# The further slots of split expert weights placed at a multiple of 128 bytes in the partition instead of 64 past one

## The chip, the core and the metric

One program runs on one core of one Trainium2 chip. The metric is the device time of one execution in microseconds (us); smaller is better. The kernel before took 1519.38 us, the median of three runs (1519.09 to 1523.42).

## What is computed

The reference is one inference step of a two-layer decoder: 256 prompt tokens and 8 sample tokens, model width 1024, all in float32. Layer 0 is a gated linear recurrence and a dense SwiGLU; layer 1 is a short convolution and a SwiGLU of 8 experts, of which each token takes 2. The change touches the experts alone:

```python
def moe_swiglu(x, router, w1, w3, w2):
    logits = (xt @ router).astype(F32)
    top_v, top_i = lax.top_k(logits, TOP_K)
    gates = jax.nn.softmax(top_v, axis=-1)
    combine = jnp.sum(jax.nn.one_hot(top_i, N_EXPERTS, dtype=F32) * gates[..., None], axis=1)
    for e in range(N_EXPERTS):
        out = out + combine[:, e:e + 1] * swiglu(xt, w1[e], w3[e], w2[e]).astype(F32)
```

with `swiglu(x, w1, w3, w2) = (silu(x @ w1) * (x @ w3)) @ w2`. w1 and w3 are 1024 x 3584 for each expert, w2 is 3584 x 1024.

## The kernel before

**Products in three parts.** Every large product is made of three TensorE products of fp32r numbers. A weight w is split into a high part (`whi`, an fp32r copy that ScalarE writes) and a low part (`wlo`, w minus the high part, which VectorE writes); the activations are split in the same way (`xgh` and `xgl`, `hth` and `htl`). The product is high x high, low weight x high activation, and high weight x low activation.

**Pieces and slots.** Weights arrive by DMA in halves of 1 MB (128 partitions x 2048 floats, 8192 bytes in each partition) into a ring of three `raw` buffers. One half is one piece. ScalarE makes the high part of a piece (L988, `hi_m`), VectorE the low part (L1174, called by `lo_m`), TensorE uses both in 12 matmuls, and then the semaphore `pieces_used` goes up by one and the slot can be written again. Up to the convolution there are three slots, in the tiles `whi` and `wlo`. For the experts there are six: three more lie in `whi2` and `wlo2`, which take space that the earlier stages no longer need. `bufs(q)` picks the slot of piece q by `MOE_SLOT = (3, 4, 0, 1, 2, 5)`, so the pieces go through slots 3, 4, 0, 1, 2, 5 and again. Slots 0 to 2 are in `whi` and `wlo`, slots 3 to 5 in `whi2` and `wlo2`.

**Order of TensorE in an expert.** In the experts the tokens are the stationary operand (128 rows of one expert) and the weights the moving one, 512 columns at a time. An expert has 7 column blocks of 512 (`FB`), and each block has six pieces: two of w1 (`up_m(0, ...)`), two of w3 (`up_m(1, ...)`) and two of w2 (`down_m`). `up_m` has its matmuls at L2495 to L2497, `down_m` at L2544. In `body` the order of a block in the loop is: the next block's w1 pieces (slots 2 and 5), four transposes of the hidden rows (`turn`, L2528), the next block's w3 pieces (slots 3 and 4), and this block's w2 pieces (slots 0 and 1). `head` begins the first expert with w1 in slots 3 and 4 and w3 in slots 0 and 1. 8 experts of 7 blocks of 6 pieces are 336 pieces and 4032 matmuls, half of them on slots 3 to 5.

**Order of the other queues.** SyncE issues the DMA of a half as soon as VectorE is through with the half that lay there (`chunk`, L362). ScalarE waits for the landing and for `pieces_used` of the piece that held the slot before, six pieces back; VectorE waits for ScalarE; TensorE waits in `piece` for `lo_done`. Each of these orders is written out by hand. Nothing else is placed in the space of `whi2` and `wlo2` during the experts. Before them it holds tiles of the earlier stages and the gain row `gffn` (128 x 1024), which is placed at `W2_AT` plus two slots.

**Addresses.** The constants, `raw`, `whi` (partition address 50304) and `wlo` (74880) are laid out one behind another; 50304 and 74880 are multiples of 128 and a slot is 8192 bytes, so slots 0 to 2 begin at multiples of 128. The last tile of the routing, `pm`, ends at 179136, which is `W2_AT` and 64 past a multiple of 128; `wlo2` follows at 203712, also 64 past. `hth_last` (152128), `htl_last` (156224), `xgh`, `xgl`, `hth` and `htl` begin 64 past a multiple too. At the end of the program `yh` (107904, a multiple of 128) and `yl` (164416, 64 past one) are the moving operand of 512 columns at L2613, with `pick` as the stationary one.

Of the kernel before, what the change touches and what calls it, by code (L numbers as in the profile page):

```python
# [33 lines left out]
def build(nc, x_prompt, x_sample, state_hgrn, state_conv, norm_mix, norm_ffn, norm_final,  # L34
# [38 lines left out]
    with ExitStack() as ctx:  # L73
# [5 lines left out]
        def size(shape, dt):  # L79
            n = 2 if dt == BF16 else 4  # L80
            for s in shape[1:]:
                n *= s
            return (n + 31) // 32 * 32
# [40 lines left out]
        def region(offset, *specs):  # L124
            out = []
            for name, shape, dt in specs:
                out.append(at(name, shape, dt, offset))
                offset += size(shape, dt)
                assert offset <= nc.sbuf_usable_end, (name, offset)
            return out, offset  # L130
# [26 lines left out]
        for g_ in range(2):  # L157
# [7 lines left out]
            for tiles, tile in ((kpad, a_), (vpad, b_), (ks, c_), (vs, d_), (vbd, e_), (ox, f_)):  # L165
# [15 lines left out]
        conv_end = o  # L181
# [17 lines left out]
            ("sel_bf", [P, TT, E], BF16), ("wt", [P, TT, E], F32),  # L199
            ("iote", [P, E], F32), ("base", [P, E], F32),  # L200
            ("cnt", [P, E], F32), ("flag", [P, NS + 8], I32), ("idx", [P, 2, TT], I32), ("pm", [P, TT, P], F32))
        W2_AT = max(o, conv_end)
        (whi2, wlo2), o = region(W2_AT, ("whi2", [P, SPLIT_M - SPLIT, PW], F32R),
                                 ("wlo2", [P, SPLIT_M - SPLIT, PW], F32R))
        (gffn,), _ = region(W2_AT + 2 * size([P, PW], F32R), ("gffn", [P, D], F32))
        (back1, back2, yrows), _ = region(raw_at, ("back1", [P, TT, D], F32),
# [2442 lines left out]
```

## Time and profile before

| | before |
|---|---|
| median of 3 runs | 1519.38 us (1519.09 to 1523.42) |
| span of the profiled execution, first to last instruction | 1517.93 us |
| TensorE matmul busy | 1491.3 us, 98% of the span |
| VectorE busy | 1237.9 us, 82% |
| ScalarE busy | 962.7 us, 63% |
| GpSimd busy | 82.7 us, 5% |
| granted TensorE clock | 0.996 of full speed over the span |
| DMA | 483.97 MB, 319 GB/s over the span |
| stage of the experts | from about 542 to 1504 us |

The page gives the span of the profiled execution and no time of its own around it; the median of the runs is 1.45 us above that span. A busy TensorE in this profile is not a TensorE at its peak: the ends of matmuls are modelled, a matmul of 512 columns is shown as some 0.39 us long while the next begins after 0.23 us, so starts have to be read, not lengths.

### The profile page before, as it was taken

The numbers are of one execution on the slowest core, as the hardware profiler recorded it, in microseconds if no ns is written. First come the engines' busy times: TensorE is split into PE (matmuls) and PEld (weight loads), VectorE is DVE, ScalarE is ACT, GpSimd is POOL, SyncE is SP. The second block draws the span as 40 slices with busy tenths as digits, with TensorE's granted clock in tenths as the row PEclk, the third lists the DMA queues.
The fourth block names the chain that finished last, engine by engine and source line by source line (L and its number), as shares of the span: only waits on it lengthen the run. The fifth ranks groups of instructions, "written<-read, shape, count | busy, mean of one in ns | idle before, by whom it ended". The sixth has DMA issues, their size and how long they took to land.

```text
span 1517.9 us, 23455 instructions
## 1 busy us (share of the span) xinstructions
PE 1491.3 (98%) x8803; PEld 1298.2 (86%) x8804; DVE 1237.9 (82%) x906; ACT 962.7 (63%) x693; POOL 82.7 (5%) x65
## 2 busy tenths in 40 slices
PE   9998999999999999999999999999999999999997
PEld 9987899999999878888888888888888888888885
DVE  6898865655578788889888888888888888888887
ACT  6634443333353577777777777777777777777774
POOL 1035100000000120000000000000000000000300
PEclk9999999999999999999999999999999999999999
DMA  9644788888555679999999999999999999999991
GB/s 318 214 135 151 268 304 297 298 306 310 188 191 174 225 257 393 395 369 384 373 365 390 368 379 373 369 389 370 374 382 370 373 384 358 387 376 369 387 396 45
DMA packets 212938, 483.97 MB, mean 319 GB/s; under 512 B 8810, under 2 KB 26314, under 8 KB 209820
## 3 DMA queue, kind: packets, MB, share of 16 engines
q1 hardware_dynamic: 209224, 473.67, 85.9%
q10 hardware_dynamic: 2388, 5.32, 0.9%
q0 software_dynamic: 1280, 4.33, 0.7%
q8 instruction: 33, 0.54, 0.1%
q14 instruction: 13, 0.11, 0.0%
HBM read 446.45 MB, written 36.87 MB: 318 GB/s over the span
## 4 chain that ended last, share of the span: by engine, by line
PE 87%; DVE 1%; issue 0%; ACT 0%; DVEq 0%
PE Q L2544 20%; PE Q L2495 14%; PE Q L2497 14%; PE Q L2496 14%; PE Q L2039 7%; PE Q L2040 7%; PE Q L2041 7%; PE Q L2528 2%; DVE wlo L1174 1%; PE Q L2474 0%; PE Q L2505 0%; ACT yrows L1149 0%; PE Q L2400 0%; PE Q L2408 0%; PE Q L2032 0%
## 5 line engine op out<-in xcount | busy, mean ns | idle before, releaser
L1174 DVE TENSOR_TENSOR wlo<-raw,whi 128x2048 fp32r<-128x2048 f32 x413 | 940.6, 2295 | 197.9 <-ACT whi L988 120.1
L988 ACT ACTIVATE whi<-raw 128x2048 fp32r<-128x2048 f32 x336 | 642.9, 1921 | 179.3 <-PE Q L2497 84.1
L2495 PE MATMUL Q<-whi,xgh 128*128 128x512 f32 x896 | 358.0, 400 | 0.0
L2497 PE MATMUL Q<-whi,xgl 128*128 128x512 f32 x896 | 352.9, 394 | 0.0
L2496 PE MATMUL Q<-wlo,xgh 128*128 128x512 f32 x896 | 352.2, 393 | 0.0
L2039 PE MATMUL Q<-xh,whi 128*128 128x264 f32 x1024 | 293.7, 287 | 5.0 <-DVEq L1285 1.8
L2040 PE MATMUL Q<-xl,whi 128*128 128x264 f32 x1024 | 291.2, 284 | 0.0
L2041 PE MATMUL Q<-xh,wlo 128*128 128x264 f32 x1024 | 289.8, 283 | 0.0
L2497 PEld LDWEIGHTS Q<-whi,xgl 128*128 128x128 f32 x896 | 168.7, 188 | 39.3
L2496 PEld LDWEIGHTS Q<-wlo,xgh 128*128 128x128 f32 x896 | 168.7, 188 | 36.5
L2495 PEld LDWEIGHTS Q<-whi,xgh 128*128 128x128 f32 x896 | 168.9, 189 | 35.5
L2039 PEld LDWEIGHTS Q<-xh,whi 128*128 128x128 f32 x1024 | 192.8, 188 | 7.5 <-issue 4.1
L2040 PEld LDWEIGHTS Q<-xl,whi 128*128 128x128 f32 x1024 | 192.8, 188 | 0.3
L2041 PEld LDWEIGHTS Q<-xh,wlo 128*128 128x128 f32 x1024 | 192.5, 188 | 0.0
L2544 PE MATMUL Q<-whi,hth 128*128 128x512 f32 x440 | 174.1, 396 | 0.0
L2544 PE MATMUL Q<-whi,htl 128*128 128x512 f32 x440 | 172.5, 392 | 0.0
L2544 PE MATMUL Q<-wlo,hth 128*128 128x512 f32 x440 | 171.1, 389 | 0.0
L920 ACT ACTIVATE whi<-raw 128x2048 fp32r<-128x2048 f32 x36 | 68.8, 1911 | 90.2 <-PE Q L2041 90.2
L683 ACT ACTIVATE whi<-raw 128x2048 fp32r<-128x2048 f32 x41 | 78.2, 1912 | 72.0 <-PE Q L2041 71.1
L2544 PEld LDWEIGHTS Q<-whi,htl 128*128 128x128 f32 x440 | 82.6, 188 | 19.3
L2544 PEld LDWEIGHTS Q<-wlo,hth 128*128 128x128 f32 x440 | 82.6, 188 | 18.2
L2544 PEld LDWEIGHTS Q<-whi,hth 128*128 128x128 f32 x440 | 82.7, 188 | 16.7
(286 smaller groups left out, 1140.4 us busy)
## 6 DMA issues: line engine op xcount, KB each, us to landing
raw<-in_moe_w SPq DMA_DIRECT2D x336, 1024.0 KB, 7.6
raw<-in_ffn_w SPq DMA_DIRECT2D x42, 1024.0 KB, 7.5
raw<-in_hgrn_w_in SPq DMA_DIRECT2D x16, 1024.0 KB, 7.3
xg_rows<-zeros SPq DMA_DIRECT2D x6, 2048.0 KB, 10.9
y_rows<-zeros SPq DMA_DIRECT2D x6, 2048.0 KB, 11.5
raw<-in_conv_w_in SPq DMA_DIRECT2D x12, 1024.0 KB, 5.5
raw<-in_hgrn_w_out SPq DMA_DIRECT2D x4, 1024.0 KB, 5.2
raw<-in_conv_w_out SPq DMA_DIRECT2D x4, 1024.0 KB, 5.0
```

Source lines behind the costliest of these rows:

```text
L683: a.activation(whi[:, buf, :], raw[:, slot, PW * half:PW * (half + 1)], ACT.Copy).then_inc(hi_done, 1)
L920: a.activation(whi[:, base % SPLIT, :], raw[:, n % RAW, PW * (base % 2):PW * (base % 2 + 1)], ACT.Copy).then_inc(hi_done, 1)
L988: a.activation(bufs(q)[0], raw[:, n % RAW, PW * (q % 2):PW * (q % 2 + 1)], ACT.Copy).then_inc(hi_done, 1)
L1174: v.tensor_tensor(low, raw[:, slot, PW * half:PW * (half + 1)], high.bitcast(F32), ALU.subtract).then_inc(lo_done, 1)
L2039: t_.matmul(out, w[wslice], xhi, start=start, stop=False, **kw)
L2040: t_.matmul(out, w[wslice], xlo, start=False, stop=False, **kw)
L2041: return t_.matmul(out, lo[wslice], xhi, start=False, stop=stop, **kw)
L2495: t_.matmul(out, xgh[:, kt, :], high[:, w], start=(kt == 0), stop=False)
L2496: t_.matmul(out, xgh[:, kt, :], low[:, w], start=False, stop=False)
L2497: mm = t_.matmul(out, xgl[:, kt, :], high[:, w], start=False, stop=(kt == DT - 1))
L2528: mm = t_.transpose(Q[0][:, 2, P * c:P * (c + 1)], hx[:, P * c:P * (c + 1)], ident[:, :])
L2544: mm = t_.matmul(out, lhs[:, f, :], rhs[:, w], start=(begin and f == 0 and lhs is hth and rhs is high), stop=(last and f == 3 and lhs is h ...
```

## The change

The start of the region that holds `whi2` and `wlo2` is rounded up to a multiple of 128. `W2_AT` goes from 179136 to 179200. `whi2`, `wlo2` and `gffn` move by 64 bytes, and nothing else does. The tiles then end at 228352, inside the usable 229368. No instruction, wait, size or order is changed.

```diff
@@ -199,7 +199,7 @@
             ("sel_bf", [P, TT, E], BF16), ("wt", [P, TT, E], F32),
             ("iote", [P, E], F32), ("base", [P, E], F32),
             ("cnt", [P, E], F32), ("flag", [P, NS + 8], I32), ("idx", [P, 2, TT], I32), ("pm", [P, TT, P], F32))
-        W2_AT = max(o, conv_end)
+        W2_AT = (max(o, conv_end) + 127) // 128 * 128
         (whi2, wlo2), o = region(W2_AT, ("whi2", [P, SPLIT_M - SPLIT, PW], F32R),
                                  ("wlo2", [P, SPLIT_M - SPLIT, PW], F32R))
         (gffn,), _ = region(W2_AT + 2 * size([P, PW], F32R), ("gffn", [P, D], F32))
```

## Rows read from the trace of the kernel before

**Rows 1.** The page: busy time by engine, then granted clock in 40 slices.

```profile
PE 1491.3 (98%) x8803; PEld 1298.2 (86%) x8804; DVE 1237.9 (82%) x906; ACT 962.7 (63%) x693; POOL 82.7 (5%) x65
...
PEclk9999999999999999999999999999999999999999
```

**Rows 2.** The page: the chain that ended last, shares of the span by line.

```profile
PE Q L2544 20%; PE Q L2495 14%; PE Q L2497 14%; PE Q L2496 14%; PE Q L2039 7%; PE Q L2040 7%; PE Q L2041 7%; PE Q L2528 2%; DVE wlo L1174 1%; PE Q L2474 0%; PE Q L2505 0%; ACT yrows L1149 0%; PE Q L2400 0%; PE Q L2408 0%; PE Q L2032 0%
```

**Rows 3.** Waits of TensorE in the whole span, the longest: total us, times, longest.

```profile
PE Q L2156 <- DVE st L1392: 3.2, 5, 1.1
PE Q L2128 <- DVE U L1365: 1.8, 1, 1.8
```

**Rows 4.** Windows: length; PE, PEld, DVE, ACT, POOL busy; clock; DMA share; GB/s.

```profile
600.00:660.00 60.00, 60.00 (x272) 49.16 (x271) 52.59 (x30) 43.81 (x29) 0.00 (x0) 1.00 1.04 390
...
720.00:1470.00 750.00, 750.00 (x3370) 613.76 (x3369) 652.75 (x366) 554.83 (x363) 14.07 (x6) 1.00 1.02 376
```

**Rows 5.** Timeline of TensorE in one block: start, length, line, tiles (see text).

```profile
810.66 0.39 PE L2495 MATMUL Q<-whi,xgh 128*128 128x512 f32 x1
...
813.41 0.40 PE L2495 MATMUL Q<-whi,xgh 128*128 128x512 f32 x1
...
816.20 0.60 PE L2528 MATMUL Q<-ident,hx 128*128 128x128 f32 x4
...
816.87 0.39 PE L2496 MATMUL Q<-wlo,xgh 128*128 128x512 f32 x1
...
822.21 0.39 PE L2544 MATMUL Q<-whi,hth 128*128 128x512 f32 x1
```

**Rows 6.** The chain in order of time, around that block: start, us, what.

```profile
788.27 5.50 PE Q L2544 x24
...
805.33 5.49 PE Q L2544 x24
...
822.37 5.50 PE Q L2544 x24
```

**Rows 7.** Timeline of TensorE, the first expert's first pieces.

```profile
542.28 0.39 PE L2496 MATMUL Q<-wlo,xgh 128*128 128x512 f32 x1
...
547.64 0.40 PE L2495 MATMUL Q<-whi,xgh 128*128 128x512 f32 x1
...
553.15 0.39 PE L2495 MATMUL Q<-whi,xgh 128*128 128x512 f32 x1
```

**Rows 8.** Timeline of TensorE, the last two pieces and the products behind them.

```profile
1498.14 0.39 PE L2544 MATMUL Q<-whi,hth_last 128*128 128x512 f32 x1
...
1500.88 0.39 PE L2544 MATMUL Q<-whi,hth_last 128*128 128x512 f32 x1
...
1503.67 0.85 PE L2613 MATMUL Q<-yh,pick 128*8 128x512 f32 x3
1504.36 0.86 PE L2613 MATMUL Q<-yl,pick 128*8 128x512 f32 x3
1505.06 0.85 PE L2613 MATMUL Q<-yh,pick 128*8 128x512 f32 x3
1505.75 0.87 PE L2613 MATMUL Q<-yl,pick 128*8 128x512 f32 x3
```

**Rows 9.** Lines L988 and L1174: ns min/median/max, first and last start in us.

```profile
L988 ACT ACTIVATE whi<-raw x336: 1895/1921/1938, 509.2 to 1487.2; 128x2048 fp32r<-128x2048 f32 x168
...
L1174 DVE TENSOR_TENSOR wlo<-raw,whi x413: 2279/2292/3376, 16.7 to 1489.3; 128x2048 fp32r<-128x2048 f32 x138
```

**Rows 10.** Waits from 620 to 1480 us: who waited for whom, us, times, longest.

```profile
DVE wlo L1174 <- ACT whi L988: 111.3, 168, 3.0
ACT whi L988 <- PE Q L2497: 79.9, 125, 0.9
ACT whi L988 <- PE Q L2544: 69.6, 85, 0.8
...
ACT whi L988 <- DMA raw<-in_moe_w: 5.8, 7, 1.5
```

**Rows 11.** The page: DMA issues of the expert weights, KB each, us to landing.

```profile
raw<-in_moe_w SPq DMA_DIRECT2D x336, 1024.0 KB, 7.6
```

## The prediction

> **What bounds the kernel now.** I read the page first: TensorE is busy for 98% of the span, and the granted clock has the digit 9 in all 40 slices, the level of 2.4 GHz [rows 1], and the chain that ended last is almost only its matmuls; the four lines of the experts, L2544 and L2495 to L2497, hold 62% of the span [rows 2]. Then the waits of TensorE: the longest of them belong to the recurrence (L2156, L2128), 3.2 us and less, and no line of the experts is in that list [rows 3]. The windows say the same: from 720 to 1470 us TensorE is busy for 750.00 of 750 us [rows 4]. So in the experts TensorE is fed in time, and their length is the number of matmuls times the distance between two starts. The other engines have room there: VectorE 652.75 and ScalarE 554.83 of the 750 us [rows 4].
>
> A busy TensorE is not a TensorE at its peak, so I then read the distances between starts, piece by piece, in the timeline, because the change alters nothing but where three of the six slots begin. In the code a piece has 12 matmuls, and the order of slots is known, so the kernel before already holds the comparison: slots 0, 1 and 2 begin at a multiple of 128 bytes, slots 3, 4 and 5 begin 64 past one.
>
> - One block of the loop [rows 5, 6]. The 24 matmuls of `down_m` (slots 0 and 1) take 5.49 to 5.50 us, 228.8 ns each. The first w1 piece (slot 2) runs from 810.66 to 813.41, 2.75 us or 229.2 ns each. The second w1 piece (slot 5), the same line and the same loop, runs from 813.41 to the transposes at 816.20, 2.79 us or 232.5 ns each. The w3 pieces (slots 3 and 4) run from their second matmul at 816.87 to 822.21: 23 distances in 5.34 us, 232.2 ns each. (The first distance there, 816.55 to 816.87, holds the tail of the transposes and is left out.)
> - The start of the first expert, with the roles changed [rows 7]. Now w1 is in slots 3 and 4: 542.28 to 547.64 is 23 distances in 5.36 us, 233.0 ns. w3 is in slots 0 and 1: 547.64 to 553.15 is 24 in 5.51 us, 229.6 ns. The slower pieces go with the slot, not with w1 or w3, or with the PSUM bank.
> - The last two pieces, when VectorE and ScalarE split nothing any more (the last split starts at 1489.3 and lasts 2.3 us [rows 9]). Slot 2 takes 1498.14 to 1500.88, 2.74 us; slot 5 takes 1500.88 to 1503.67, 2.79 us, with the same stationary tiles [rows 8]. So it isn't a collision with what writes the other slots.
> - Two tiles outside the slots, both moving operands of 512 columns, three matmuls at a time: `yh`, on a multiple of 128, 0.69 us (1503.67 to 1504.36, and 1505.06 to 1505.75); `yl`, 64 past one, 0.70 us (1504.36 to 1505.06) [rows 8]. That is a difference of 3 ns for a matmul, at the limit of what two decimals tell, but in the same direction, and `yl` at 164416 lies below the region of the change.
>
> My reading is that a moving operand of 2048 bytes in a partition costs 3 to 4 ns more when it starts 64 past a multiple of 128. All chunks of a slot are 2048 bytes apart, so all 12 matmuls of a piece have the same offset.
>
> **The change part by part.** It adds and removes no instruction, wait or byte of traffic. It moves three things by 64 bytes.
>
> 1. What TensorE reads. 56 blocks have one piece each in slots 3, 4 and 5. For slots 3 and 4: 23 distances x (232.2 - 228.8) = 78 ns. For slot 5: 12 x (232.5 - 228.8) = 44 ns. Together 122 ns a block, x 56 = 6.9 us. The distance left out holds one further matmul of slot 3, 56 x 3.4 ns = 0.2 us if it gains too; I take 7.0 us. The lower end: each of the two stretches is known to 10 ns at either end, so 20 ns less on a block gives 102 x 56 = 5.7 us. The upper end: the 233.0 ns of the first pieces against the 228.3 ns of slot 2 at the end (2.74 us / 12), 4.7 x 36 x 56 = 9.5 us; I don't take it, since one block in the loop is shown at 232.2 and the block repeats with a period of 17.06 and 17.04 us [rows 6].
> 2. What ScalarE and VectorE write. 168 high parts and 168 low parts go to the moved slots. No row separates slots; all high parts are within 1895 to 1938 ns around 1921, and the low parts have a median of 2292 [rows 9]. If all of the spread of L988 were due to the offset, it would be 43 ns x 168 = 7.2 us more or less on ScalarE, spread over 960 us in which it is idle for a quarter of the time [rows 4]. It is off the path either way: TensorE never waits for `lo_done` in the experts [rows 3]. I take nothing. Without that cover it would be at most those 7.2 us.
> 3. `gffn`, 64 bytes further, read by GpSimd and VectorE once for each of 3 row tiles before the experts. Of an operation of this width the trace shows nothing that depends on 64 bytes, and if half of the 3.4 ns x 12 of a whole piece were lost or won on each, it would be some 0.1 us. I take nothing.
>
> What is late next? A block that lasts 17.05 us would last 16.93. Its six transfers are 6.29 MB (six of 1024 KB [rows 11]), so the rate wanted goes from 369 to 372 GB/s, and with the rows of tokens and results, 376 [rows 4] goes to about 379. The same queues moved 390 GB/s from 600 to 660 us, while they caught up after the routing [rows 4]. In the loop ScalarE's copies wait mostly for TensorE to free a slot (79.9 + 69.6 us, 210 times) and seldom for a landing (5.8 us, 7 times) [rows 10], so the data lie there before they are wanted. VectorE needs 6 x 2.29 us [rows 9] and two small operations, some 15 of the 16.93 us. Nothing becomes the bound through 0.12 us.
>
> The sum: span 1517.93 - 7.0 = 1510.9 us. The median of the runs is 1.45 us above the span of the profile, so I predict 1512.4 us, a gain of 0.46%.
>
> Two pages of the Trainium skill were weighed. "TensorE: Matmul & The Clock Gate", section "Back-to-back issue gap", gives the distance of two matmuls as the columns over the clock and a fixed 2.5 ns, with no term for where the moving operand begins; it would be 215.8 ns for every slot, and the change would be worth nothing: 1519.4 us. The rows at 228.8 and 232.3 ns differ from it in the level, and in that they depend on the slot. "SBUF — State Buffer", section "Operand start alignment", asks only for a multiple of the element size and says that this is about legality and that nothing was timed, so it has no speed for either place. I go by the rows.
>
> **The rivals.** Each is a case with a time of its own.
> - *The region, not the offset: no change.* Slots 3 to 5 are also the only ones above 179136. If matmuls that read the far part of the partition are slow, 64 bytes change nothing and the time stays 1519.4. For it: slots and region go together in every piece. Against it: `yl`, which lies lower and is slow, though by a difference near the resolution [rows 8]. Chance 0.10. (The section of the Trainium skill named above would end at the same time; the rows at two levels speak against it.)
> - *Half of it.* The speed goes with the offset, but something fed to TensorE keeps part of it: transfers that never got above the present 376 GB/s, or a coarser boundary than 128 that only some slots meet (179200 is a multiple of 256, 50304 is not). 3.5 us, 1515.9. Against: the 390 GB/s, and that slots 0 to 2 are the fast ones though they start 128 past a multiple of 256. Chance 0.05.
> - *Slower: the writers.* If SBUF serves TensorE's reads and the two writers best when they are 64 bytes apart, then six slots with the same offset would put every read beside writes of its own offset. It decides if the reads of slots 0 to 2, which now have a writer at the other offset for part of the time, fall to the rate of slots 3 to 5: 168 x 12 x 3.5 ns = 7.1 us more, 1526.4. Against it: by the order in the code slot 2 is read while slots 0 and 1 are refilled, all on multiples of 128, and it is as fast as any (229.2 ns) [rows 5]. Chance 0.03.
>
> **How the numbers follow.** The whole gain has 0.82, half of it 0.05, no change 0.10, slower 0.03. The prediction is the likeliest, 1512.4. Its own bounds are 1509.9 (9.5 us) and 1513.7 (5.7 us); the lower is a bound from the slowest and the fastest rows at once, and I stop at 1510.5. Upward the range takes in the half gain at 1515.9 with the spread of a run and ends at 1516.5. A measurement of this kernel can tell about 0.3%, 4.6 us, from no change, so faster means below 1514.8. The whole gain falls there but for 0.02: faster 0.80. Half a gain, no change, and the rest count as the same: 0.17. Slower 0.03.
>
> **What would show it.** After: the 23 distances of slots 3 and 4 in 5.26 us instead of 5.34, slot 5's piece in 2.75 us instead of 2.79, blocks 16.93 us apart in the chain of waits; the first pieces of the first expert at 229 and not 233 ns; slots 0 to 2 and `yl` unchanged; the waits of ScalarE for landings still a few us. If slots 3 to 5 stay at 232 ns, step 1 is wrong and it was the region. If they fall and the blocks don't, look for a wait of TensorE on `lo_done`, which would make the transfers the new bound. If slots 0 to 2 rise, it is the writers.

## The result and the profile after

The changed kernel takes 1522.61 us (median of 22 runs, 1521.25 to 1525.6); the kernel before takes 1519.68 us beside it (22 runs, 1518.35 to 1523.53). The ratio is 1.0018, 95% interval 1.0012 to 1.0024: 2.9 us slower. The forecast was 1512.4 us.

First the page of the changed kernel, busy time of the engines, and then the chain in order of time with the two products of `down_m` (slots 0 and 1) that enclose one block (start, us, what):

```profile
PE 1495.6 (98%) x8803; PEld 1298.3 (85%) x8804; DVE 1238.6 (81%) x906; ACT 961.6 (63%) x693; POOL 82.3 (5%) x65
```

```profile
792.16 5.50 PE Q L2544 x24
809.26 5.50 PE Q L2544 x24
```

The picture is that of [rows 1] and [rows 6]: TensorE is busy throughout, slots 0 and 1 take 5.50 us as before. But the block lasts 17.10 us instead of 17.05. The timeline of TensorE in the block behind it shows where (compare [rows 5]):

```profile
814.60 0.39 PE L2495 MATMUL Q<-whi,xgh 128*128 128x512 f32 x1
...
817.34 0.40 PE L2495 MATMUL Q<-whi,xgh 128*128 128x512 f32 x1
...
820.15 0.60 PE L2528 MATMUL Q<-ident,hx 128*128 128x128 f32 x4
...
820.83 0.40 PE L2496 MATMUL Q<-wlo,xgh 128*128 128x512 f32 x1
...
826.20 0.39 PE L2544 MATMUL Q<-whi,hth 128*128 128x512 f32 x1
```

Slot 2 is unchanged (814.60 to 817.34, 2.74 us). Slot 5 takes 2.81 us where it took 2.79, and the 23 distances of slots 3 and 4 take 5.37 us, 233.5 ns each, where they took 5.34. The moved slots were to become 3.5 ns faster and became 1 ns slower. Over all 336 pieces, each matmul taken from its start to the next start on TensorE and the distances of 260 ns and more at transposes left out, the means are:

| slot | before | after |
|---|---|---|
| 3 | 232.11 ns | 233.52 ns |
| 4 | 232.24 | 233.29 |
| 5 | 232.81 | 233.59 |
| 0 | 229.35 | 229.49 |
| 1 | 228.91 | 228.88 |
| 2 | 228.89 | 228.89 |

From the first to the last matmul of the experts it is 963.82 us instead of 961.48, 2.34 us more. That is the larger part of the 2.9 us. The span of this profile is longer by 5.6 us; the other 3.3 lie ahead of the experts, which begin at 545.28 instead of 541.95. The windows from 100 to 200 us of before and of after (length; PE, PEld, DVE, ACT, POOL busy; clock; DMA share; GB/s):

```profile
100.00:200.00 100.00, 90.83 (x904) 83.38 (x903) 85.26 (x121) 43.70 (x51) 34.41 (x23) 1.00 0.63 204
```

```profile
100.00:200.00 100.00, 90.55 (x879) 82.91 (x879) 84.82 (x120) 41.99 (x50) 34.19 (x23) 0.97 0.61 200
```

The clock was granted at 0.97 there instead of 1.00, and 25 fewer matmuls were done: in two stretches of 3.4 us, at 119 and 146 us, the clock was at the level of 1.2 GHz instead of 2.4. No row ties this to the change. The profiles of e3_low_plus64 and e5_all_moved_64 below have the same two stretches, before has one, at 12 us, and the other four kernels with experts have one, at some 143 us. The runs of one kernel spread over some 3 us, and each profiled run with two such stretches is among the longer ones of its kernel, so the length of the experts' stage is given beside the times (961.48 us in two kernels with equal distances, before and e5_all_moved_64).

### The profile page after: what moved, and what is told of

Same layout as the page of the kernel before. It is cut to its first block, busy times and chain, and to the rows that moved or that the text cites. A ratio compares the mean times of both kernels' runs of the same rounds, so it can differ in the third digit from the quotient of the medians.

```text
span 1523.5 us, 23455 instructions
## 1 busy us (share of the span) xinstructions
PE 1495.6 (98%) x8803; PEld 1298.3 (85%) x8804; DVE 1238.6 (81%) x906; ACT 961.6 (63%) x693; POOL 82.3 (5%) x65
## 4 chain that ended last, share of the span: by engine, by line
PE 86%; DVE 1%; issue 0%; ACT 0%; DVEq 0%
PE Q L2544 20%; PE Q L2495 14%; PE Q L2496 14%; PE Q L2497 14%; PE Q L2039 7%; PE Q L2040 7%; PE Q L2041 7%; PE Q L2528 2%; DVE wlo L1174 1%; PE Q L2474 0%; PE Q L2505 0%; ACT yrows L1149 0%; PE Q L2400 0%; PE Q L2408 0%; PE Q L2032 0%
## 5 line engine op out<-in xcount | busy, mean ns | idle before, releaser
L1174 DVE TENSOR_TENSOR wlo<-raw,whi 128x2048 fp32r<-128x2048 f32 x413 | 941.4, 2297 | 200.2 <-ACT whi L988 122.8
L988 ACT ACTIVATE whi<-raw 128x2048 fp32r<-128x2048 f32 x336 | 642.0, 1918 | 182.0 <-PE Q L2497 86.5
```

Source lines behind the costliest of these rows:

```text
L988: a.activation(bufs(q)[0], raw[:, n % RAW, PW * (q % 2):PW * (q % 2 + 1)], ACT.Copy).then_inc(hi_done, 1)
L1174: v.tensor_tensor(low, raw[:, slot, PW * half:PW * (half + 1)], high.bitcast(F32), ALU.subtract).then_inc(lo_done, 1)
```

## The experiments

The table gives all kernels that compute the experts' stage, and is for all that follows; the other four kernels run groups of matmuls alone. "Past 256" is the address of a tile modulo 256. The stationary tiles are `xgh`, `xgl`, `hth` and `htl`, which agree in it; so do `whi` and `wlo`, and `whi2` and `wlo2`. The distance is that of the moving operand minus that of the stationary one, modulo 256; it was found in the first three runs and tested in the others. The column of ns leaves out slots 0, 3 and 5, which stand behind a change of slots or behind the transposes and read up to 4.5 ns off the level of their distance for it.

| kernel | past 256: stationary, slots 0-2, slots 3-5 | distance: 0-2, 3-5 | ns: slots 1 and 2, slot 4 | experts' stage | median |
|---|---|---|---|---|---|
| before | 64, 128, 192 | 64, 128 | 228.9, 232.2 | 961.48 us | 1519.7 |
| after | 64, 128, 0 | 64, 192 | 228.9, 233.3 | 963.82 | 1522.6 |
| e2_w2_plus128 | 64, 128, 64 | 64, 0 | 228.9, 226.7 | 955.69 | 1514.0 |
| e3_low_plus64 | 192, 192, 64 | 0, 128 | 226.7, 231.8 | 959.53 | 1518.7 |
| e5_all_moved_64 | 128, 192, 0 | 64, 128 | 228.9, 232.2 | 961.48 | 1522.0 |
| e6_all_at_256 | 0, 128, 0 | 128, 0 | 233.3, 226.7 | 962.05 | 1519.9 |
| e7_distance_0 | 128, 128, 128 | 0, 0 | 226.7, 226.7 | 947.70 | 1505.1 |
| e9_distance_64 | 64, 128, 128 | 64, 64 | 228.9, 228.9 | 955.15 | 1513.3 |

### e1_reads: the reads alone

The theory of the offset had fallen with the result; its rival of the region was left, and a third, that the moving and the stationary operand disturb each other. The kernel fills the partition and runs groups of 24 matmuls from chosen places:

```diff
+            for i in range(N): mm = nc.tensor.matmul(*args(i, 16384, 10240), start=(i == 0), stop=(i == N - 1))
+            for i in range(N): mm = nc.tensor.matmul(*mats(i, (179136, 203712), (152128, 156224)), start=(i == 0), stop=(i == N - 1))
```

`args(i, moving, stationary)` gives the addresses at which the two operands begin; `mats` takes high and low tiles of each in the order of the kernel.

> This kernel computes nothing of the reference: it fills the partition with ones and runs groups of 24 matmuls of 512 columns on an otherwise idle core, one group for each place of the moving operand and of the stationary one (the outputs are copies of inputs). What counts is the distance between two starts in each group. The theory of the offset (64 past a multiple of 128 is slow, wherever it lies): a level near 229 ns for every moving operand at a multiple of 128 and 232 to 233 ns for 64 past, in both regions. It has lost in the changed kernel, where the moved slots went from 232.4 to 233.5 ns. The theory of the region: with any stationary operand, the distance goes from about 229 to about 233 ns at one address of the moving operand between 107904 and 164416 and stays there. The theory of the common part: the distance is about 233 ns only where the moving and the stationary operand lie in the same part of the partition, so with the stationary operand at 10240 the low places are the slow ones and with it at 152064 the high ones. If all groups lie within 0.5 ns, the reads alone don't make the difference and something else that runs in the kernel does.

The timeline of TensorE merges each group into a row (start, length, line); the time of a group is the difference of two starts. L76 to L99 and L100 to L124 are the scans with the moving operand from 16384 or 24576 to 212992 and the stationary one at 10240, then 152064. L161 to L169 are `mats` with slots 0, the further slots of before, and those of after, each with the stationary tiles at 152128 and 156224 (as in the kernel), at 152064 and 156160, and at 10240 and 14336:

```profile
80.11 5.60 PE L76 MATMUL Q<-big 128*128 128x512 f32 x24
...
210.67 5.60 PE L100 MATMUL Q<-big 128*128 128x512 f32 x24
...
346.67 5.60 PE L125 MATMUL Q<-big 128*128 128x512 f32 x24
...
546.82 5.67 PE L161 MATMUL Q<-big 128*128 128x512 f32 x24
552.33 5.73 PE L162 MATMUL Q<-big 128*128 128x512 f32 x24
557.90 5.75 PE L163 MATMUL Q<-big 128*128 128x512 f32 x24
563.48 5.75 PE L164 MATMUL Q<-big 128*128 128x512 f32 x24
569.07 5.76 PE L165 MATMUL Q<-big 128*128 128x512 f32 x24
...
580.27 5.76 PE L167 MATMUL Q<-big 128*128 128x512 f32 x24
585.87 5.63 PE L168 MATMUL Q<-big 128*128 128x512 f32 x24
591.34 5.60 PE L169 MATMUL Q<-big 128*128 128x512 f32 x24
```

Both scans run at 5.44 us for a group at every place (L76 to L100: 130.56 us for 24 groups; L100 to L125: 136.00 us for 25), 226.7 ns. No region is slow and no common part is: both theories are out. The same holds at other distances: a moving operand 64 bytes further on takes 229.4 ns for a matmul in the low part (49216) and in the high part (179264). Everything that works through the other engines is out as well, since slow and fast groups appear here with TensorE alone. L161 is slot 0 with the kernel's stationary tiles: 5.51 us. The same moving tiles with a stationary one 64 bytes lower (L162) take 5.57. The tiles of before (L164) take 5.59, those of after (L167) 5.60; L164 is 233.0 ns, where the same pair in the kernel reads 232.2, and e8 comes back to that. And those of after with the stationary tiles 64 bytes lower (L168) take 5.47. So the same moving operand, at 179200, is the slowest or nearly the fastest by where the stationary one lies.

### e2_w2_plus128 and e3_low_plus64: other starts in the kernel

```diff
-        W2_AT = max(o, conv_end)
+        W2_AT = max(o, conv_end) + 128
```

> The region of the further slots begins at 179264, 64 past a multiple of 128 as before, but 128 bytes further on. If only the place within 128 bytes matters for the second, small effect (the 1 ns by which the moved slots got slower), slots 3 to 5 read at 232.1 to 232.8 ns as before, and the time is that of before within 0.5 us. If it is the place within 256 bytes or more, the slots take another value, up to 1.2 ns from that of before, which is 2.4 us.

It is 5.8 us faster than before: 1514.04 us (5 runs), ratio 0.9959, 0.9945 to 0.9972. The further slots are still 64 past a multiple of 128, which by my prediction is the slow place, and slot 4 reads at 226.7 ns, faster than any slot of before. Both branches of the expectation were wrong, since both looked at the moving operand's place only. Around one of its blocks the chain shows slots 0 and 1 in 5.51 us and 16.94 us from block to block, instead of 5.49 and 17.05:

```profile
787.33 5.51 PE Q L2544 x24
804.27 5.51 PE Q L2544 x24
```

```diff
+        top[0] += 64
         whi = keep("whi", [P, SPLIT, PW], F32R)
         wlo = keep("wlo", [P, SPLIT, PW], F32R)
+        top[0] += 64
```

> Slots 0 to 2 begin 64 past a multiple of 128, all that lies behind them is moved by 128 bytes, so slots 3 to 5 are at 179264, 64 past, too. By the theory of the offset slots 0 to 2 go from 228.9 to above 232 ns and the kernel takes 6 to 7 us more. By the theory of the region they stay at 228.9 within 0.5 ns, and the kernel is at the time of the run with the further slots at 179264. By the theory of the common part it is the same, since the stationary tiles stay in the high part. The dense layer and the convolution use the slots as the stationary operand; if its offset mattered there, their stage (up to about 490 us) would change.

1518.73 us (11 runs), ratio 0.9993, 0.9984 to 1.0002; the stage of the experts is 1.95 us shorter. Slots 1 and 2, now 64 past a multiple of 128, went down from 228.9 to 226.7 ns, and slot 0, behind the slots at another distance, up from 229.4 to 230.6. The stages ahead of the experts show no effect: the experts begin at 545.36 us, and at 545.28 and 545.42 in the two other kernels whose profile has the two slow stretches. In the groups of e1 and in these two kernels one rule fits the levels to about 1 ns: what counts is the distance of the two operands modulo 256, or modulo 512, which these data don't tell apart.

### e4_distance_scan

> Again groups of 24 matmuls on an otherwise idle core and nothing of the reference (outputs are copies of inputs). The theory of the distance: what counts is the difference between the partition addresses of the moving and the stationary operand, modulo 256 bytes: 226.7 ns at 0, 228.8 at 64, 232.6 at 128, 233.3 to 234 elsewhere. Then the scan of the moving operand over 1024 bytes in steps of 32 repeats itself four times, and moving the stationary operand instead gives the mirror image. If the period is 512, it repeats twice and the distances of 256 and 768 are slow. The groups of 264 columns ask whether the stages with short products depend on it as well; if the load of 128 columns sets their pace, they show one level. Of the groups with two alternating pairs, the one with matmul i's moving operand 128 away from its own stationary operand but 0 from the next one tells which of the two loads it is: below 229 ns if it is the load of the next stationary operand that meets the running stream, near 232 ns if it is the matmul's own.

L87 to L95 are the moving operand at 49152 and then 32, 64 ... 256 bytes on, the stationary one at 10240:

```profile
73.92 5.60 PE L87 MATMUL Q<-big 128*128 128x512 f32 x24
79.36 5.77 PE L88 MATMUL Q<-big 128*128 128x512 f32 x24
84.97 5.67 PE L89 MATMUL Q<-big 128*128 128x512 f32 x24
90.47 5.77 PE L90 MATMUL Q<-big 128*128 128x512 f32 x24
96.08 5.76 PE L91 MATMUL Q<-big 128*128 128x512 f32 x24
101.68 5.78 PE L92 MATMUL Q<-big 128*128 128x512 f32 x24
107.30 5.76 PE L93 MATMUL Q<-big 128*128 128x512 f32 x24
112.90 5.76 PE L94 MATMUL Q<-big 128*128 128x512 f32 x24
118.50 5.63 PE L95 MATMUL Q<-big 128*128 128x512 f32 x24
123.96 5.77 PE L96 MATMUL Q<-big 128*128 128x512 f32 x24
```

The groups take 5.44, 5.61, 5.50, 5.61, 5.60, 5.62, 5.60, 5.60 and 5.46 us, and so on four times up to 1024 bytes: the period is 256. The first matmuls of a group still feel the group before, so the levels are taken from the later part of each, over whole repetitions of its pattern: 226.7 ns at 0, 228.9 at 64 and 233.3 to 234.3 at every other step of 32. Moving the stationary operand instead gives the mirror image, as expected (228.9 ns with it 192 further on, 233.3 with it 64), but for the distance of 128, which is 232.4 ns here and 233.3 in the other scan. Groups of 264 columns lie between 120.0 ns (distances 0 and 192) and 126.7 (96) over the same scan, so short products depend on it too, in another pattern; what that is worth in the kernel wasn't tried by itself. The two alternating pairs came to 228.4 ns with each matmul's own operands at distance 0 and 230.0 with the next one's. Neither is near a level of the simple theory, so this part was inconclusive.

### e5_all_moved_64: the same start as in the change, all distances kept

```diff
-        top = [(nc.sbuf_base + 63) // 64 * 64]
+        top = [(nc.sbuf_base + 63) // 64 * 64 + 64]
```

> Everything in the partition moves by 64 bytes: the further slots now begin at 179200, exactly as in the change, and slots 0 to 2 begin 64 past a multiple of 128. No distance between two tiles changes. The theory of the distance: slots 3 to 5 at 232.1 to 232.8 and slots 0 to 2 at 228.9 to 229.4 ns, the time that of the kernel before within 0.5 us. By a theory of places (a start of 179200 is slower than one of 179136 by itself) the further slots go to 233.4 ns as in the changed kernel and the kernel takes 2 to 3 us more.

The further slots begin at 179200 as in the changed kernel, and each slot reads as before to 0.01 ns (232.11, 232.24, 232.82; 229.35, 228.91, 228.89). The stage of the experts takes 961.48 us, as before. The chain shows the block of [rows 6]:

```profile
791.74 5.50 PE Q L2544 x24
808.79 5.49 PE Q L2544 x24
```

17.05 us. The median, 1522.02 (11 runs, 1518.77 to 1523.15), is not what was expected, but its interval holds no change (ratio 1.0007, 0.9998 to 1.0016). In the profile the experts begin 3.47 us later than before, with the two stretches of lower clock told of above, and last as long as before. What brings these stretches on, and whether the move has a part in it, isn't shown.

### e6_all_at_256: every start at a round address, wrong distances for slots 0 to 2

```diff
-        R0 = top[0]
+        R0 = top[0] + 192
...
-        W2_AT = max(o, conv_end)
+        W2_AT = (max(o, conv_end) + 255) // 256 * 256
```

> The region of the later stages begins 192 bytes further on, so the stationary tiles of the experts and the further slots begin at multiples of 256, slots 0 to 2 stay 128 past one. The theory of the distance: slots 3 to 5 (distance 0) at 226.7 ns but for the first matmuls behind a change of slots, slots 0 to 2 (distance 128) at 232.3; 11 us less and 7 us more, so 1515 to 1516 us. By a theory of places slots 0 to 2 stay at 228.9 and the kernel comes to the 1514.0 of the run with the further slots at 179264, or stays at 1522 if a multiple of 128 is what made slots 3 to 5 slower.

1519.93 us (11 runs), ratio 1.0004, 0.9995 to 1.0014: no gain, though the stationary tiles and slots 3 to 5 begin at multiples of 256 and slots 0 to 2 at multiples of 128. Slots 0 to 2, which nobody moved, went from 228.9 to 233.3 ns, and slot 4 to 226.7: the direction of the theory. The sum was too good by some 4 us. The distance of 128 cost 233.3 ns here and not 232.3, and slots 3 and 5 behind a change of distance reached only 230.9 and 228.3. The next kernels avoid the changes, and e8 comes back to the 233.3.

### e7_distance_0 and e9_distance_64: one distance for all slots

```diff
-        R0 = top[0]
+        R0 = top[0] + 64
...
-        W2_AT = max(o, conv_end)
+        W2_AT = (max(o, conv_end) + 127) // 256 * 256 + 128
```

> The region of the later stages begins 64 bytes further on, and the further slots at 179328, so the stationary tiles of the experts and all six slots are 128 past a multiple of 256 and every distance is 0. The theory of the distance: 226.7 ns in all six slots, no slower matmuls behind a change of slots, 4032 matmuls with 2.2 ns (slots 0 to 2) and 5.6 ns (slots 3 to 5) less than before, 15 to 16 us, so about 1504 us. A theory of places would give nothing like it: no slot would begin anywhere that a slot of before, of the change or of the other runs has not been slower at.

1505.06 us (5 runs, 1504.38 to 1508.69), ratio 0.991, 0.9896 to 0.9923: 14.5 us faster than before, with the same instructions. The timeline of TensorE, to be read like [rows 5]:

```profile
805.76 0.39 PE L2495 MATMUL Q<-whi,xgh 128*128 128x512 f32 x1
...
808.48 0.39 PE L2495 MATMUL Q<-whi,xgh 128*128 128x512 f32 x1
...
811.20 0.60 PE L2528 MATMUL Q<-ident,hx 128*128 128x128 f32 x4
```

Slot 2 and slot 5 take 2.72 us each; slots 0 and 1 take 5.44 us in the chain, and a block 16.81:

```profile
783.67 5.44 PE Q L2544 x24
800.48 5.44 PE Q L2544 x24
```

The stage of the experts is 13.8 us shorter, where 15 to 16 were expected of the time. Equal distances don't remove every slow matmul: slot 3, behind the transposes, reads at 229.7 ns and slot 5 at 227.1, since its last matmul before them takes 231. And the feeding holds. From 720 to 1450 us (windows), and in the waits of ScalarE (us in total, times, longest us), that for a landing:

```profile
720.00:1450.00 730.00, 730.00 (x3327) 604.79 (x3326) 642.40 (x361) 546.53 (x358) 13.71 (x6) 1.00 1.02 381
```

```profile
ACT whi L988 <- DMA raw<-in_moe_w: 15.0, 18, 2.3
```

The transfers move 381 GB/s instead of 376 [rows 4], ScalarE waits for a landing 18 times instead of 7 [rows 10], and TensorE waits for nothing in the experts.

Then all slots at the distance of 64, the stationary tiles left where they were:

```diff
-        W2_AT = max(o, conv_end)
+        W2_AT = max(o, conv_end) + 192
```

> The further slots begin at 179328, 128 past a multiple of 256 like slots 0 to 2, and the stationary tiles stay 64 past one, so all six slots have the distance 64. The theory of the distance: 228.9 ns in all six, no slower matmuls behind a change of slots, 3.4 to 3.9 ns x 2016 = 7 to 8 us less than before, 1512 us. That is the gain which the prediction expected of the multiple of 128. 179328 is a multiple of 128 as the change's 179200 is, so a theory of multiples of 128 gives the 1522 us of the change.

1513.33 us (5 runs), ratio 0.9955, 0.9942 to 0.9969. The further slots begin at 179328, a multiple of 128 as in the change, and read at 228.9 (slot 4), 229.3 (slot 5) and 229.7 ns (slot 3, behind the transposes). That is nearly the gain the prediction worked out, 6.3 us where it had 7.0, by a start 128 bytes beyond the one of the change. A block takes 16.94 us, where the prediction had 16.93:

```profile
786.22 5.49 PE Q L2544 x24
803.16 5.49 PE Q L2544 x24
```

### e8_which_load and e10_odd_one: what meets what

> Groups of 24 matmuls on an idle core, nothing of the reference. First a grid: moving and stationary operand each 0, 64, 128 and 192 past a multiple of 256, every group behind one with distance 0. If the distance alone sets the level, the four pairs of one distance agree within 0.5 ns; if the two places matter by themselves, the distance of 128 shows between 232 and 233.4 ns as it did so far. Then stationary operands 0, 32 and 128 past in turn, which are at slow distances from each other, with the moving operand equal to the matmul's own stationary one, to the next one's, or to the one's after that. The one that comes to about 227 ns names the load that meets the running stream; the two others should be near 233. If none of them is below 230, the distance acts in another way than by one load meeting one stream.

In the grid, with levels taken as in e4, distance 0 is 226.7 ns for all four pairs, 64 is 228.9 and 192 is 233.3. At 128 it is 232.4 ns for three pairs and 233.3 for the moving operand 128 past and the stationary one at a multiple of 256, which is the pair of e6. But the places don't decide it by themselves. In e1 that same pair, in the kernel's order of high and low tiles (L163), repeats seven distances from 228 to 241 ns with a mean of 232.4, and the pair of the kernel before (L164) has 237 and 230 in turn, 233.3, where the kernel itself reads 232.2. At the distance of 128 the stream has two patterns, and what picks one is open. Then the three stationary operands in turn; L132 and L133 have the moving operand equal to the matmul's own, L135 and L136 to the next one's, L138 and L139 to the one's after that:

```profile
344.27 5.74 PE L132 MATMUL Q<-big 128*128 128x512 f32 x24
349.85 5.74 PE L133 MATMUL Q<-big 128*128 128x512 f32 x24
355.44 5.65 PE L134 MATMUL Q<-big 128*128 128x512 f32 x24
360.93 5.66 PE L135 MATMUL Q<-big 128*128 128x512 f32 x24
366.43 5.66 PE L136 MATMUL Q<-big 128*128 128x512 f32 x24
371.92 5.65 PE L137 MATMUL Q<-big 128*128 128x512 f32 x24
377.40 5.74 PE L138 MATMUL Q<-big 128*128 128x512 f32 x24
382.98 5.73 PE L139 MATMUL Q<-big 128*128 128x512 f32 x24
```

5.58 us, 5.50 and 5.58: 232.6, 228.9 and 232.4 ns. By the mark set beforehand, below 230, it is the next matmul's stationary operand that matters most here, but 228.9 isn't 226.7, and the alternating pairs of e4 lean the other way (228.4 with the own operands at distance 0, 230.0 with the next one's).

> Groups of 24 matmuls on an idle core, nothing of the reference, all with distance 0 but for every sixth (i = 3, 9, 15, 21), whose stationary operand, moving operand or both lie 64, 128 or 192 further on. If a stream is slowed by the load of the next matmul's stationary operand, an odd stationary operand lengthens the distance that begins one matmul before it (i = 2) and an odd moving operand the one that begins with it (i = 3), and with both odd by the same amount both are lengthened. If it is the matmul's own load that counts, both odd by the same amount costs nothing. If several distances in a row change, the two streams keep a memory of more than one matmul, and no single pair explains the level. The test with two pairs in turn had come out at 228.4 and 230.0 ns, between the levels, which the simple theory of the next load doesn't give.

The timeline merges these groups, so the single starts are read from the trace behind it. With distance 0 everywhere they are 226 to 227 ns apart. With the stationary operand of matmul 3 alone 128 further on, the distances from the start of matmul 2, and from that of matmul 3, are 232 and 234 ns. With the moving operand of matmul 3 alone 128 on, only the one from matmul 3 is longer, 235 ns. So with 128 a stationary operand acts on the distance before its matmul, as the theory of the next load has it, and on its own as well, which that theory doesn't explain. With the stationary operand 64 or 192 on, the distance before stays at 226 ns, against that theory, and the effect lasts: 236, 228, 232, 231 for 64, and then 227.

Other cases last longer. The moving operand 64 on gives 237, 241, 224, 231, 235, 229 up to the next odd one, and with both odd by 128 the distances are back at 226 to 227 ns only eleven matmuls after the last odd one begins. These last eight are 233, 236, 224, 231, 236, 228, 233 and 231, and the same row of numbers stands in the kernel where the distance changes (slot 5 of e2_w2_plus128 after slot 2: 234, 231, 233, 236, 224, 231, 236, 228, 233, 231, 226, 233). That is a memory of several matmuls: no single pair explains a level, and it fits that pieces behind a change of distance are slow for some matmuls. How the two reads interlock in the hardware is open.

## Why the prediction was wrong, point by point

- **What bounds the kernel: right.** The time of the experts is matmuls times the distance of their starts, in every kernel here, down to 947.70 us.
- **The comparison of slots: the numbers were right, the cause was not.** The two speeds, 228.8 and 232.3 ns, are real and belong to the slots. The step that failed is the reading that ended it, and with it the term of 7.0 us in step 1: "a moving operand of 2048 bytes in a partition costs 3 to 4 ns more when it starts 64 past a multiple of 128". All comparisons of the first three items had the stationary tiles at one place, 64 past a multiple of 256, so a start and a distance to the stationary tile couldn't be told apart, and both addresses stood in the text. What the runs show in its place is the distance of the two operands modulo 256: 179136 is at distance 128 and 179200 at distance 192, and 233.3 to 233.6 ns instead of 232.1 to 232.8 is what that costs. With the same start of 179200 and the old distances (e5_all_moved_64) the slots read as before.
- **The fourth item, `yl`, misled.** It was to separate offset and region. `pick` and `yl` are both 64 past a multiple of 256, distance 0, so by the rule found it should be the faster one. It stands behind `yh`, at distance 64, and slot 5 of e2_w2_plus128 goes through the same change with 234, 231 and 233 ns for its first three matmuls, which is 0.70 us, as [rows 8] have it. That it is this here was not tried by itself, but in e7_distance_0, where `yh`, `yl` and `pick` all lie 128 past a multiple of 256, the starts of all twelve matmuls are 226 to 227 ns apart, `yl` like `yh`. A difference of three matmuls at the resolution of the rows was given too much weight.
- **Step 1, the size.** The step has 7.0 us less, and the stage took 2.34 us more: 616 x 1.41 + 672 x 1.05 + 672 x 0.78 ns = 2.1 us in the matmuls of slots 3, 4 and 5, the rest at transposes and in slot 0. The other 0.6 us of the 2.9 between the medians are not explained by a row.
- **Step 2, the writers: right.** ScalarE's high parts have a mean of 1918 ns where they had 1921, VectorE's low parts 2297 where they had 2295, and TensorE waits for neither in the experts. **Step 3** shows nothing.
- **What is late next: right, and tested harder than the change did.** In e7_distance_0 a block lasts 0.24 us less than before and TensorE still doesn't wait.
- **The rivals.** The region is ruled out by e1_reads. The half gain by a coarser boundary is ruled out by the changed kernel itself, whose moved slots begin at a multiple of 256 and got slower, and by e5_all_moved_64, where the same start reads as before. The other ground for a half, transfers that don't keep up, is out too: TensorE waits for nothing in the experts. The slower case came out on its side, with 2.9 us instead of 7.1 and another mechanism: not writers beside reads, but the place of one operand of TensorE against the other. That slots 0 to 2 kept 228.9 ns rules the writers out. No rival said that the effect lies between two operands of the same engine, though the code shows a load beside every matmul.
- **The rule of the Trainium skill.** "TensorE: Matmul & The Clock Gate", section "Back-to-back issue gap", has no term for a place and would have given no change, which is nearer to the measured 0.2% than the forecast but not for its reason. The prediction took its 215.8 ns for 512 columns and left out that the section calls this the gap of an isolated matmul and gives about 131 ns for a stream of loads and matmuls. Neither level appears here: the best distance of these 512-column fp32r matmuls, each with a load of its own, is 226.7 ns.

## What to carry to other kernels

Where TensorE is back to back and each matmul has its own load, compare the address of the moving operand with that of the stationary one, modulo 256, before aligning either; equal is best (226.7 ns for 512 columns of fp32r), the moving operand 64 bytes further on is next (228.9), the stationary one 64 further on is among the slow ones (233.3), and one middling distance for all buffers of a ring did slightly better than the best one for some of them (the stage took 955.15 us in e9_distance_64 and 955.69 in e2_w2_plus128). Rounding a start up moves only one end of the distance. And when two groups in a trace differ in speed, list everything in which they differ together, the relation to the other operand too, before the change is built on one of them. Other types, and streams that keep one load for several matmuls, were not run.

## What the runs showed of the hardware

- Start to start, 512 columns of fp32r, other engines idle, clock at 2.4 GHz: 226.7 ns at distance 0 modulo 256, 228.9 at 64, 233.3 at 192, 232.4 or 233.3 at 128, and 233.3 to 234.3 at odd multiples of 32 (e4, e8). It doesn't depend on the part of the partition (50 places at distance 0, e1).
- 264 columns: 120.0 to 126.7 ns over the same scan (e4).
- The pace has a memory: matmuls with odd operands change up to eleven distances from their start on (both operands 128 further on, e10).
- The Trainium skill says in "SBUF — State Buffer", section "Who interferes with whom", that TensorE has two independent read ports, one for the moving operand and one for the loads. In these groups, with all other engines idle, the pace changes by 7.6 ns (226.7 to 234.3) with the place of one operand against the other, so for speed the two reads are not independent. That they meet in the ports or behind them is not shown.
